# Moving the down-bias spread and the small output products to the middle of the expert loop

## The reference, cut to what matters

```
x = x + moe(rmsnorm(x))                 # 32 experts, top 4, d_ff 1024
x = x + sigmoid(rmsnorm(x) @ w_ple_gate) * (p @ w_ple)      # p: 264 x 256
# one expert e, on the tokens that chose it:
gu   = x @ w_gu[e] + b_gu[e]            # 1024 -> 2048
hmid = (clip(up, -7, 7) + 1) * (gate * sigmoid(1.702 * gate))   # gate = min(gu_g, 7)
y    = (hmid @ w_down[e] + b_down[e]) * router_gate
```

## Time and profile before

| | |
|---|---|
| median of 3 runs | 1390.29 us (1388.4 to 1392.27) |
| profiled execution, its own time | 1391.61 us |
| its span | 1389.8 us |
| PE busy | 1328.8 us (96%) |
| DVE busy | 373.9 us (27%) |
| ACT busy | 226.3 us (16%) |
| DMA moved | 530.55 MB, mean 382 GB/s |
| chain that ended last, by engine | PE 55%, DMA 33%, ACTq 4%, DVE 4%, ACT 2% |

### The profile page before, as it was taken

How to read it: one execution, slowest core, us unless ns; L and a number is a source line. 1 busy time by engine, 2 the same in 40 slices (tenths; PEclk the granted TensorE clock), 3 DMA queues, 4 the chain that set the end, 5 groups by cost and what they waited for, 6 DMA issues and landing times.

```text
span 1389.8 us, 15637 instructions
## 1 busy us (share of the span) xinstructions
PE 1328.8 (96%) x6626; PEld 673.4 (48%) x6626; DVE 373.9 (27%) x528; ACT 226.3 (16%) x407; POOL 17.3 (1%) x33
## 2 busy tenths in 40 slices
PE   7999999999989999999999999999999999999987
PEld 6787878888853333333333333333323233333336
DVE  3069714221241122122222221212222121211224
ACT  3312145322031101101101011010101001011011
POOL 0000111000000000000000000000000000000000
PEclk9999999999998999999999999999999999999999
DMA  9889994988997999999999999999999999999970
GB/s 388 312 278 402 328 387 161 295 321 318 412 371 267 419 428 427 426 429 428 428 426 429 430 427 427 429 429 429 425 429 429 429 427 426 428 428 427 427 307 33
DMA packets 50564, 530.55 MB, mean 382 GB/s; under 512 B 6077, under 2 KB 6221, under 8 KB 21781
## 3 DMA queue, kind: packets, MB, share of 16 engines
q1 hardware_dynamic: 35252, 470.42, 81.1%
q10 hardware_dynamic: 13841, 54.68, 10.6%
q0 software_dynamic: 1424, 4.76, 1.6%
HBM read 525.08 MB, written 58.38 MB: 420 GB/s over the span
## 4 chain that ended last, share of the span: by engine, by line
PE 55%; DMA 33%; ACTq 4%; DVE 4%; ACT 2%; issue 1%; SPq 0%; POOL 0%; DVEq 0%
DMA ring<-in_wexp 27%; PE PS L848 26%; PE PS L579 13%; DMA HL<-in_wexp 5%; ACTq L410 4%; PE PS L863 3%; PE PS L1024 2%; PE PS L903 2%; DVE ring L1354 1%; PE PS L884 1%; PE PS L854 1%; PE PS L658 1%; ACT Zb L1234 1%; PE PS L593 1%; DMA cst<-in_cst 1%
## 5 line engine op out<-in xcount | busy, mean ns | idle before, releaser
L848 PE MATMUL PS<-ring,Zb 128*64 128x512 f32 x2304 | 517.6, 599 | 24.3 <-DMA ring<-in_wexp 22.6
L848 PEld LDWEIGHTS PS<-ring,Zb 128*64 128x64 f32 x2304 | 159.5, 137 | 345.4 <-issue 294.1
L579 PE MATMUL PS<-HL,ring 128*128 128x264 f32 x1024 | 232.2, 386 | 0.0
L579 PEld LDWEIGHTS PS<-HL,ring 128*128 128x128 f32 x1024 | 193.1, 190 | 32.6 <-issue 0.4
L1601 DVE COPY attT<-PS 64x512 f32<-64x512 f32 x32 | 21.9, 684 | 327.5 <-PE PS L848 327.5
L1242 ACT ACTIVATE Zb<-Zb 128x512 f32<-128x512 f32 x32 | 20.2, 630 | 443.3 <-DVE Zb L1579 443.3
L848 PE MATMUL PS<-Zb 128*64 128x512 f32 x384 | 89.0, 606 | 0.8 <-issue 0.4
L848 PE MATMUL PS<-HL,Zb 128*64 128x512 f32 x384 | 87.1, 595 | 2.0 <-DMA HL<-in_wexp 1.6
L1569 DVE TENSOR_TENSOR xc<-xc,PS 128x528 f32<-128x528 f32 x68 | 47.6, 701 | 103.8 <-PE PS L903 94.9
L1234 ACT ACTIVATE Zb<-PS 128x512 f32<-128x512 f32 x32 | 19.1, 597 | 330.7 <-PE PS L869 330.7
L903 PE MATMUL PS<-Zb,attT 128*128 128x264 f32 x240 | 69.5, 412 | 0.0
(11 more groups left out here) (240 smaller groups left out, 886.9 us busy)
## 6 DMA issues: line engine op xcount, KB each, us to landing
ring<-in_wexp SPq DMA_DIRECT2D x144, 2048.0 KB, 32.6
Zb<-in_wexp SPq DMA_DIRECT2D x24, 2048.0 KB, 32.9
HL<-in_wexp SPq DMA_DIRECT2D x24, 2048.0 KB, 34.0
ring<-in_win SPq DMA_DIRECT2D x16, 2048.0 KB, 12.4
out_kvs<-in_cache ACTq DMA_DIRECT2D x8, 4032.0 KB, 33.3
out_kvs<-in_cache ACTq DMA_DIRECT2D x8, 1984.0 KB, 21.8
ring<-in_kt SPq DMA_DIRECT2D x2, 2048.0 KB, 16.4
ring<-in_vt SPq DMA_DIRECT2D x2, 2048.0 KB, 12.0
```

What stands on the lines that cost most here:

```text
L579: last = mm(PS[:, z_bank(n), 0:T], w[:, k, t * P:(t + 1) * P], hT[:, k, :], start=(k == 0), stop=(k == KT - 1))
L848: last = mm(PS[CAP * h:CAP * (h + 1), bank, :], src[:, k, f:f + CAP], w[:, k, h * CH:(h + 1) * CH], start=(not seeded and slot % 2 == 0 an ...
```

## The change

The bias spread leaves pair 0, where no spread stands any more. In pair 6 (MID = 3, the first pair of the fourth group of four experts) each spread of pair 5's result becomes two products per bank: first the bias product (start), then the result (stop), so VectorE adds once. The gate transposes and ScalarE's copy move to pair 6; spread 0 of that pair stands after g1 instead of after g0. The eight small tiles move from pairs 12, 13, 14 (3, 3, 2) to pairs 6 and 7 (4, 4). The counts of `added` and `c_mm` start one pair later (four less). PE's loop becomes two: pair 2 to 5 and 8 to 13, with pairs 0, 1, 6, 7, 14, 15 written out; ScalarE's becomes pairs 0 to 5 and 8 to 14, with 6, 7 and 15 written out. VectorE's loop stays.

```diff
-PLE = ((0, 3), (3, 6), (6, 8))
+PLE = ((0, 4), (4, 8))
+MID = 3
...
-            def spread(j, q):
-
-                if not (isinstance(j, int) and j == 0 and q == 0):
-                    pe.wait_ge(S.added, 4 * j + q)
+            def spread(j, q, bias=False):
+
+                if not (isinstance(j, int) and j == 1 and q == 0):
+                    pe.wait_ge(S.added, 4 * j + q - 4)
                 for t in range(2):
                     c = (2 * q + t) * P
-                    if isinstance(j, int) and j == 0:
-                        last = mm(PS[:, 2 + t, 0:T], bdn[:, c:c + P], gateT[:, :], start=True, stop=True)
-                    else:
-                        last = mm(PS[:, 2 + t, 0:T], yb[:, c:c + P], gpickT[:, :], start=True, stop=True)
+                    if bias:
+                        mm(PS[:, 2 + t, 0:T], bdn[:, c:c + P], gateT[:, :], start=True, stop=False)
+                    last = mm(PS[:, 2 + t, 0:T], yb[:, c:c + P], gpickT[:, :], start=not bias, stop=True)
                 last.then_inc(S.c_mm, 1)
...
                 if prev:
-                    if isinstance(j, int) and j == 0:
+                    pe.wait_ge(S.y_ev, n)
+                    pe.wait_ge(S.goT_ok, j)
+                    if bias:
                         pe.wait_ge(S.gate_ok, 1)
                         for b, (t0, nt) in enumerate(BLK):
                             last = nc.tensor.transpose(PS[0:E, 7, t0:t0 + nt], gate[0:nt, b, :], ident[0:nt, 0:nt])
                         last.then_inc(S.gt_mm, 1)
                     else:
-                        pe.wait_ge(S.y_ev, n)
-                        pe.wait_ge(S.goT_ok, j)
                         spread(j, 0)
                 arrived(r, q, 1)
                 half_product(0, xgT, r, 1).then_inc(S.g1_mm, 1)
                 if prev:
-                    if isinstance(j, int) and j == 0:
+                    if bias:
                         pe.wait_ge(S.gt_ok, 1)
                         pe.wait_ge(S.bdn_in, 16)
-                        spread(j, 0)
-                    spread(j, 1)
+                        spread(j, 0, bias)
+                    spread(j, 1, bias)
...
                 if ple is not None:
-                    pe.wait_ge(S.added, 4 * j + 4)
+                    pe.wait_ge(S.added, 4 * j)
                     ple_tiles(*ple)
...
-            def pair(q, odd, following=True, ple=None):
+            def pair(q, odd, prev=True, following=True, ple=None, bias=False):
                 j = 2 * q + odd
-                block_(2 * j, j, 0, 2 * odd, q)
+                block_(2 * j, j, 0, 2 * odd, q, prev=prev, bias=bias)
                 block_(2 * j + 1, j, 1, 2 * odd + 1, q, prev=False, following=following, ple=ple)
 
-            pair(0, 0)
+            pair(0, 0, prev=False)
             pair(0, 1)
-            with pe.Fori(1, E // 4 - 2) as q:
+            with pe.Fori(1, MID) as q:
                 for odd in range(2):
                     pair(q, odd)
-            pair(E // 4 - 2, 0, ple=PLE[0])
-            pair(E // 4 - 2, 1, ple=PLE[1])
-            pair(E // 4 - 1, 0, ple=PLE[2])
+            pair(MID, 0, ple=PLE[0], bias=True)
+            pair(MID, 1, ple=PLE[1])
+            with pe.Fori(MID + 1, E // 4 - 1) as q:
+                for odd in range(2):
+                    pair(q, odd)
+            pair(E // 4 - 1, 0)
             pair(E // 4 - 1, 1, following=False)
...
+            with act.Fori(0, 2 * MID) as j:
+                block_(2 * j, j, 0)
+                block_(2 * j + 1, j, 1)
             act.wait_ge(S.gt_mm, 1)
             A(gateT, PS[0:E, 7, 0:T], ACT.Copy).then_inc(S.gt_ok, 1)
-            with act.Fori(0, E // 2 - 4) as j:
+            for odd in range(2):
+                j = 2 * MID + odd
+                block_(2 * j, j, 0)
+                block_(2 * j + 1, j, 1, ple=PLE[odd])
+            with act.Fori(2 * MID + 2, E // 2 - 1) as j:
                 block_(2 * j, j, 0)
                 block_(2 * j + 1, j, 1)
-            for i in range(3):
-                j = E // 2 - 4 + i
-                block_(2 * j, j, 0)
-                block_(2 * j + 1, j, 1, ple=PLE[i])
...
             def block_(i, n, j, o, prev=True, following=True, alone=False, last=False):
 
                 first = isinstance(n, int) and n == 0
-                if prev and not first:
+                if prev:
                     add_spread(j, 0)
...
                 if prev:
-                    if first:
-                        add_spread(j, 0)
                     add_spread(j, 1)
                     add_spread(j, 2)
...
-            block_(0, 0, 0, 0)
+            block_(0, 0, 0, 0, prev=False)
```

More of the change, by code:

```diff
@@ L908, in arrived, with block_ @@
                 pe.wait_ge(arrival(r, s), 16 * (3 * q + (6 * r + s) // DEPTH + 1))
-            def block_(n, j, o, r, q, prev=True, following=True, ple=None):
+            def block_(n, j, o, r, q, prev=True, following=True, ple=None, bias=False):
                 arrived(r, q, 0)
@@ L937, in block_ @@
                 if prev:
-                    spread(j, 2)
+                    spread(j, 2, bias)
                 arrived(r, q, 3)
@@ L941, in block_ @@
                 if prev:
-                    spread(j, 3)
+                    spread(j, 3, bias)
                 if ple is not None:
-                    pe.wait_ge(S.added, 4 * j + 4)
+                    pe.wait_ge(S.added, 4 * j)
                     ple_tiles(*ple)
@@ L970, in spread_all @@
                 pe.wait_ge(S.goT_ok, j)
-                pe.wait_ge(S.added, 4 * j)
+                pe.wait_ge(S.added, 4 * j - 4)
                 pe.wait_ge(S.gmin, 2 * j)
@@ L975, in spread_all @@
                     if q >= 2:
-                        pe.wait_ge(S.added, 4 * j + q - 1)
+                        pe.wait_ge(S.added, 4 * j + q - 5)
                     if q == 2 and halves:
@@ L1017, in finish @@
                     if m == 3:
-                        pe.wait_ge(S.added, 2 * E + 4)
+                        pe.wait_ge(S.added, 2 * E)
                     if m == 7:
@@ L1026, in finish @@
                     last.then_inc(S.pg_mm, 1)
-            further(pe, apart, finish, after=lambda n: pe.wait_ge(S.added, 2 * n + 4), step=2)
+            further(pe, apart, finish, after=lambda n: pe.wait_ge(S.added, 2 * n), step=2)
         @block.scalar
@@ L1287, in finish @@
                 for k in range(KT):
-                    act.wait_ge(S.added, 2 * E + 1 + k // 2)
+                    act.wait_ge(S.added, 2 * E - 3 + k // 2)
                     A(hT[:, k, :], xc[:, k, :], ACT.Copy, scale=feat[:, k, FGP:FGP + 1]).then_inc(S.hp_ok, 1)
@@ L1294, in finish @@
                     A(sgp[:, m, :], sgp[:, m, :], ACT.Sigmoid).then_inc(S.pg_sig, 1)
-            further(act, apart, finish, after=lambda n: act.wait_ge(S.added, 2 * n + 4))
+            further(act, apart, finish, after=lambda n: act.wait_ge(S.added, 2 * n))
         @block.vector
@@ L1565, in add_spread @@
             def add_spread(j, q, at=2):
-                v.wait_ge(S.c_mm, 4 * j + q + 1)
+                v.wait_ge(S.c_mm, 4 * j + q - 3)
                 x = xc[:, 2 * q:2 * q + 2, :]
@@ L1617, in shift_ranks @@
             def shift_ranks(c):
-                v.wait_ge(S.added, 2 * c * E + 4)
+                v.wait_ge(S.added, 2 * c * E)
                 TS(rank, rank, -float(CAP), None, ALU.add).then_inc(S.shifted, 1)
@@ L1635, in finish @@
                 done[0] = links
-                v.wait_ge(S.added, 2 * E + 4)
+                v.wait_ge(S.added, 2 * E)
                 link(TT(lt[:, :, :], xc[:, :, :], xc[:, :, :], ALU.mult))
@@ L1653, in finish @@
                 ple_out(KT - 1)
-            further(v, apart, finish, before=shift_ranks, after=lambda n: v.wait_ge(S.added, 2 * n + 4))
+            further(v, apart, finish, before=shift_ranks, after=lambda n: v.wait_ge(S.added, 2 * n))
         @block.gpsimd
```

## The result

The changed kernel takes 1382.88 us (median of 8 runs, 1382.19 to 1386.06), the kernel before 1390.21 in the same comparison: a ratio of 0.995, interval 0.9939 to 0.996, or 7.3 us. The forecast was 1383.3.

What follows compares the result with a forecast made beforehand. The prediction took the expert weight stream, with holes only during expert 0, to bound the kernel. Its terms, -7.0 + 0 + 0 us, took the 1390.29 us median to 1383.3, with 8 in 10 between 1381.0 and 1387.7.

Steps and rivals of the forecast that it cites:

- What bounds: Whole kernel: the expert weight stream sets the end, at 4.945 us per transfer, with holes only during expert 0.
- Pair 0: Expert 0: without transposes, spreads and the wait, PE reaches the next rows 8.2 us earlier; down products start at 438.48.
- the spare time of the fifth transfer: Weight stream in expert 0: after the change the fifth transfer could start 1.2 us before its turn.
- The stream: Weight stream during expert 0: holes of 3.35 and 3.65 us close, so the stream ends 7.0 us earlier.
- The queue, piece by piece: Weight transfers: each lands 4.945 us after the one before, or 7.6 us after issue if nothing is ahead.
- Pair 6: Bias work arriving there: products 4.6 us, transposes 0.43, wait up to 1.71, slow half product 1.70; costed at 0.
- The cover: Pairs 6 and 7: at most 16.3 us of PE work, hidden by a 26 us stock; cost 0.
- below 428 GB/s anywhere from pair 6 on: Sign in the new trace: the prediction is wrong if the DMA rate drops under this from pair 6.
- A: Expert 0: the stream doesn't fill with two transfers in flight; gain 5.4 us, 1384.9; chance 0.13.
- B: Expert 0: held elsewhere, by late bias rows of expert 1, so nothing is gained; 1390.3; chance 0.06.
- C: From pair 6: PE falls behind for good and the DMA gets holes; 1397 at 40 us of lag; chance 0.06.
- D: Expert 0's early holes don't matter, as other transfers set the end; 1390.3; chance 0.05.

Runs made afterwards that it cites:

- e1: Against the changed kernel, only the bias half: the small output products stay in pairs 12, 13 and 14; 1383.7 us, ratio 0.9955 to the kernel before.
- e3: Kernel before, with pair 0's second spread in PSUM banks 6 and 7, so PE skips the wait for VectorE; 1386.5 us, ratio 0.9975 to the kernel before.
- e4: Changed kernel plus eleven useless products (7.1 us) in expert 0 between u1 and the next rows; 1388.3 us, ratio 0.9983 to the kernel before.
- e9: The changed kernel itself, measured again in a later group; 1383.4 us, ratio 0.9945 to the kernel before.
- e5: Changed kernel with each small output product of pairs 6 and 7 computed three times; 1383.9 us, ratio 0.9954 to the kernel before.
- e6: Changed kernel with each small output product of pairs 6 and 7 computed six times; 1404.0 us, ratio 1.0094 to the kernel before.
- e2: Kernel before, with only the small output products moved to pairs 6 and 7, bias spread still in pair 0; 1389.9 us, ratio 0.9999.
- e7: Changed kernel with the bias product moved to pair 15 and the small output products to pairs 14 and 15; 1393.2 us, ratio 1.0015 to the kernel before.
- e12: Changed kernel plus three useless products after the last u1 only; 1382.9 us, ratio 0.9941 to the kernel before.
- e8: Changed kernel plus useless products in PE's gaps, six before expert 0 and three after the last u1; 1381.0 us, ratio 0.9934 to the kernel before.

## Why the prediction was right, step by step

- *What bounds:* right. The end follows the stream of weights; e1, e3 and e4 move it by moving holes in the stream during expert 0.
- *Pair 0:* PE was to gain 8.2 us up to the gather; it gained 8.7 (10.26 for 18.97), since g1, u0 and u1 take 3.42 each in an unbroken row, not 3.6, and the rows up to the down products 4.17 instead of 4.31. The down products start 14.43 us behind the first release, 15.08 in the forecast; the 0.65 went into the spare time of the fifth transfer, not to the end.
- *The stream:* right in the sum: 7.0 us forecast, 6.9 from release to the landing of the fourth piece of expert 31, and e3 gives the first half by itself (3.5). The spare time of the fifth transfer was put at 1.2 us; with the 0.65 it comes to 1.85, and e4 shows 1.8.
- *The queue, piece by piece:* right only in the sum, and that with some luck. It puts two whole gaps into the stream before, ahead of the third and the fifth piece. The landings show five wide steps instead, 6.0 to 7.3 us: the second, fourth and sixth piece, each issued when just one other was on its way, landed 6.0, 7.3 and 6.2 us behind it, where the queue has 4.945. So the fourth piece landed 28.4 us behind the release, where the queue has 25.8. In the changed kernel it is the first piece that comes later than the queue has it, 8.8 us after its issue instead of 7.6, and from there on the pace holds. By the tenth piece the queue is 1.1 us early before the change (59.1 for 60.2) and 0.8 early after it (52.1 for 52.9); the two errors cancel in the difference, which nothing in the prediction gave a reason to expect.
- *Pair 6:* the term of the bias products was sized too small, 4.6 us; a quarter with bias takes four times 0.64 = 2.56 instead of 1.09, so 5.9. The wait for VectorE was 0.78 (755.74 + 0.66 to 757.18) instead of up to 1.71, and no half product was slow. The small products took 7.5, not 7.9. That makes 14.6 us, within the 16.3 given. But this profile was the mild case: in the other nine traces that carry the bias in pair 6 the same wait of about 0.8 us is followed by the low clock. In e9, the changed kernel again, spread products take up to 1.18 us and u0 4.89 (windows as in the earlier trace rows, the first in e9, the second in the first profile of the changed kernel):

```profile
760.00:764.00 4.00, 4.00 (x8) 1.50 (x6) 0.91 (x2) 0.63 (x1) 0.00 (x0) 0.50 0.98 418
```
```profile
760.00:764.00 4.00, 4.00 (x19) 1.19 (x15) 0.56 (x1) 0.00 (x0) 0.00 (x0) 1.00 0.99 422
```

  From the end of g1 to the end of u0 it is 12.77 us in e9 and 9.57 in the first profile. With these 3.2 us pairs 6 and 7 get 17.8, over the upper bound, since the prediction allowed for a slow half product but not for slow spreads ahead of it. All of it is hidden in both.
- *The cover:* no cost, as said; waits for weights came back at 967.86, the fourth piece of expert 19 (72 landings before 1323.71), so in pair 9, two pairs earlier than the latest one named. e5 and e6 bear out the stock of about 26 us. The sign "below 428 GB/s anywhere from pair 6 on" was set too tight: windows of 20 us from 740 to 980 read 424 to 431, and the kernel before has slices of 425 too. The landings decide here: from 769.7 to 972.7 they are 4.95 us apart in the mean, none more than 5.4.
- *Rivals:* A (a stream that doesn't fill with few in flight) fell with the windows of 429 to 431 GB/s; B (bias rows late) with the gather's bias rows running on at once; C needs over twice the work (e6), and e2, which has the same two loops, loses nothing by them; D fell with e1 and e3, whose gains reach the end.

## What to carry to other kernels

Where a stream of transfers sets the end, look for the stretch in which it stands still; there alone PE's time counts, and work can be moved from there to any place that has both a stock of transfers under way and enough stretches behind it to regain the time. A queue of three numbers (issue times, landing pace, shortest landing) told the end of e1 to e7 to within 2 us, though not each landing and not the place of e6's first hole; the landings of single transfers are in the trace and should be read first. Compare traces from a mark behind what both have in common, not whole spans; and read a second profile of the same kernel before a stretch is called free of the low clock.

## What was not expected of the hardware

- The same instructions ahead of expert 0 ran at different clocks from execution to execution: the window 408 to 416 had a granted clock of 0.52 in e9, 0.72 in e12, 0.96 in e4 (and 1.00 in e8, which fills the gaps there), and the time from SP's issue behind the router's logits to the first release went from 16.9 us (changed kernel) to 20.5 (e9). In the profiles this moves the first release by up to 3.6 us, with which the spread of the runs would agree. Why the clock fell earlier in one than in the other is open. The same holds in pair 6: after a wait of some 0.8 us the clock fell in nine traces and stayed up in one. Ahead of the slow u0 of the kernel before PE had waited 1.71 us; in e3, without that wait, it did not fall.
- The mean rate over the 16 DMA engines is not the pace of landings: 2 MB in 4.945 us is 424 GB/s, the windows say 428. In e5 a window fell without cost to the end:

```profile
880.00:900.00 20.00, 19.82 (x101) 7.33 (x97) 2.77 (x4) 2.12 (x5) 0.00 (x0) 1.00 0.90 368
```

  2.8 us of mean rate are missing there, yet the landings kept on: eleven of them from 875.3 to 930.7, 5.04 us apart in the mean, which loses 1.0 us, and the fourth piece of expert 31 lands 902.5 us after the first release (902.8 in the changed kernel). So it is the landings that say whether a low mean rate costs anything. Why the rate can fall while the landings keep their pace is open; the view gives the 16 engines only together.
- Two products that alternate between 32 and 128 rows of weights into the same bank took 0.64 us each, where two products of one kind in a row (four records) take 1.09, 0.55 each. The spreads differ in accumulation as well as in rows, and no run separates the two.
